# Hidden rows of three low-rank products kept in their PSUM banks

## The reference, cut to what matters

```python
def rwkv7_time_mix(h, ...):
    xx = token_shift(h) - h
    xr, xw, xk, xv, xa, xg = (h + xx * mu[j] for j in range(6))
    r = xr @ wr
    w_log = -jax.nn.softplus(-(w0 + jnp.tanh(xw @ w1) @ w2)) - 0.5
    k = xk @ wk
    v = xv @ wv
    a = jax.nn.sigmoid(a0 + (xa @ a1) @ a2)
    g = jax.nn.sigmoid(xg @ g1) @ g2
```

## Time and profile before

| what | value |
|---|---|
| time, median of 3 | 2699.92 us |
| lowest and highest | 2696.75 and 2700.97 us |
| the profiled execution | 2697.75 us |
| its span, first to last instruction | 2696.0 us |
| busy: PE, DVE, ACT, POOL | 2557.6, 1278.4, 740.1, 1479.3 us |
| mean granted clock of PE | 0.97 of full speed |

### The profile page before, as it was taken

One profiled execution on the slowest core, in us unless ns is written; L12 is line 12 of the kernel. 1 busy time (PEld: TensorE's weight loads), 2 busy tenths in 40 slices (PEclk: granted clock), 3 DMA queues, 4 the chain that ended last, 5 costly groups with the idle time before them and its releaser, 6 DMA issues. The chain is left out here.

```text
span 2696.0 us, 36707 instructions
## 1 busy us (share of the span) xinstructions
PE 2557.6 (95%) x15042; PEld 2039.6 (76%) x15042; DVE 1278.4 (47%) x1862; ACT 740.1 (27%) x1395; POOL 1479.3 (55%) x482
## 2 busy tenths in 40 slices
PE   5899988999999999999999998999799999999998
PEld 4677777788888796667888887777676568878787
DVE  7737336775662141453845526855075625131211
ACT  4643322231120212452311212322323423011210
POOL 3663632577777665205777772443373037754674
PEclk9999988999999999999999998999899999999999
DMA  6221424566562222103555522222253336222121
GB/s 268 98 82 53 128 78 169 237 236 230 222 230 96 87 101 78 54 1 136 219 203 219 211 100 99 90 106 94 94 187 111 125 148 237 105 77 71 70 97 75
DMA packets 89903, 358.80 MB, mean 133 GB/s; under 512 B 27288, under 2 KB 41112, under 8 KB 52384
## 3 DMA queue, kind: packets, MB, share of 16 engines
q1 hardware_dynamic: 64848, 227.12, 23.3%
q10 hardware_dynamic: 24912, 129.64, 12.8%
HBM read 317.66 MB, written 39.06 MB: 132 GB/s over the span
## 5 line engine op out<-in xcount | busy, mean ns | idle before, releaser
L499 POOL TENSOR_TENSOR whi<-wraw,con_sb 128x2048 fp32r<-128x2048 f32 x166 | 600.5, 3617 | 1002.8 <-PE ps L552 662.3
L501 POOL TENSOR_TENSOR wlo<-wraw,whi 128x2048 fp32r<-128x2048 f32 x166 | 782.6, 4715 | 13.0
L552 PE MATMUL ps<-hh,whi 128*128 128x512 f32 x952 | 372.9, 392 | 3.3 <-DVE hl L1930 3.3
L552 PE MATMUL ps<-hl,whi 128*128 128x512 f32 x952 | 371.5, 390 | 0.0
L552 PE MATMUL ps<-hh,wlo 128*128 128x512 f32 x952 | 371.4, 390 | 0.0
L552 PEld LDWEIGHTS ps<-hh,whi 128*128 128x128 f32 x952 | 179.4, 188 | 44.2 <-issue 3.7
L2155 DVE TENSOR_TENSOR midl<-rsq,midh 128x512 fp32r<-128x512 f32 x64 | 153.9, 2409 | 114.4 <-ACT midh L2112 114.4
L552 PEld LDWEIGHTS ps<-hh,wlo 128*128 128x128 f32 x952 | 179.4, 188 | 37.6
L552 PEld LDWEIGHTS ps<-hl,whi 128*128 128x128 f32 x952 | 179.5, 189 | 36.7
L552 PE MATMUL ps<-midh,whi 128*128 128x512 f32 x512 | 199.9, 391 | 0.0
L552 PE MATMUL ps<-midh,wlo 128*128 128x512 f32 x512 | 199.9, 390 | 0.0
(11 more groups left out here) (475 smaller groups left out, 4820.6 us busy)
## 6 DMA issues: line engine op xcount, KB each, us to landing
wraw<-wst SPq DMA_DIRECT2D x162, 1024.0 KB, 4.8
cond_w<-wcond ACTq DMA_DIRECT2D x68, 1024.0 KB, 4.8
first_w<-wcond SPq DMA_DIRECT2D x8, 1024.0 KB, 19.4
mod_w<-wcond SPq DMA_DIRECT2D x8, 1024.0 KB, 14.0
d_v<-ssb ACTq DMA_DIRECT2D x4, 1536.0 KB, 5.6
d_s<-ssb ACTq DMA_DIRECT2D x4, 1536.0 KB, 5.4
sld<-d_s SPq DMA_DIRECT2D x4, 1536.0 KB, 8.0
vld<-d_v SPq DMA_DIRECT2D x16, 384.0 KB, 3.9
```

The source lines that it names most:

```text
L499: pool.tensor_tensor(whi[:, s], wraw[:, f], C("zero").broadcast_to([P, BLK]), ALU.add).then_inc(sem("w_high"), 1)
L501: pool.tensor_tensor(wlo[:, s], wraw[:, f], whi[:, s].bitcast(F32), ALU.subtract).then_inc(w_split, 1)
L552: o = e.matmul(ps[:, b, :nt], w[:, k, mc], x[:, k0 + k, t0:t0 + nt], start=first and k == 0 and j == 0, stop=final and k == nk - 1 and j == 2)
```

## The change

The hidden rows no longer go to SBUF in full precision. ACT applies its function in place, from the bank to the same bank, then copies the bank's content rounded into `hidh` or `sgh`; DVE makes `hidl` or `sgl` from the bank and the high part. The bank is given back by DVE's subtraction (`hidden_low` raises `acc_free`), no longer by ACT's read. `hid` and `hidg` are gone, and with them ACT's two waits on `hid_ready`. PE, ahead of w2, waits for the banks of results 8 and 9 to be given back, which stands for both `hidl`.

```diff
-        hid, hidh, hidl = tiles("hid", 0, 1), tiles("hidh", 2, 1, F32R), tiles("hidl", 3, 1, F32R)
-        hidg, ksq = tiles("hidg", 0, 2), tiles("ksq", 0, 2)
+        hidh, hidl = tiles("hidh", 2, 1, F32R), tiles("hidl", 3, 1, F32R)
+        ksq = tiles("ksq", 0, 2)
...
                 full("g1", 1, 256, 5)
-                pe.wait_ge(*hid_ready.at(2))
+                for n in range(2):
+                    pe.wait_ge(*read_done(KT + n))
                 block_of(pe, firsts["w2"][1], 0, hidh, hidl, 1, BLK, mn=3)
...
-                def hidden_low(n, x, lo, hi):
+                def hidden_low(n, lo, hi, rows=slice(0, P)):
+                    b = (KT + n) % 3
                     dve.wait_ge(*hid_high.at(n + 1))
-                    dve.tensor_tensor(lo, x, hi.bitcast(F32), ALU.subtract).then_inc(*hid_ready.inc())
+                    dve.tensor_tensor(lo, ps[rows, b], hi.bitcast(F32), ALU.subtract).then_inc(acc_free[b], 1)
...
-                    hidden_low(n, hid[rr, 0], hidl[rr, 0], hidh[rr, 0])
+                    hidden_low(n, hidl[rr, 0], hidh[rr, 0], rr)
                 mixing_all(2, 1)
                 for n in range(2):
-                    hidden_low(2 + n, hidg[:, n], sgl[:, n], sgh[:, n])
+                    hidden_low(2 + n, sgl[:, n], sgh[:, n])
...
-                def hidden(x, func, hi, rows=slice(0, P)):
-                    read_out(x, func, rows=rows)
-                    act.wait_ge(*AC.last())
-                    act.activation(hi, x, ACT.Copy).then_inc(*hid_high.inc())
+                def hidden(func, hi, rows=slice(0, P)):
+                    b = bank()
+                    act.wait_ge(*AC.need(acc_ready))
+                    act.activation(ps[rows, b], ps[rows, b], func).then_inc(*hid_made.inc())
+                    act.wait_ge(*hid_made.at(hid_made.made))
+                    act.activation(hi, ps[rows, b], ACT.Copy).then_inc(*hid_high.inc())
+                    AC.up(acc_free[b])
...
                 hidden_half(1, ACT.Copy)
-                act.wait_ge(*hid_ready.at(2))
                 for n in range(2):
                     high(3)
-                    hidden(hidg[:, n], ACT.Sigmoid, sgh[:, n])
+                    hidden(ACT.Sigmoid, sgh[:, n])
                 high(2)
...
-                act.wait_ge(*hid_ready.at(4))
```

More of the change, by code:

```diff
@@ L846, in program @@
             mix_high, mix_ready = signal("mix_high"), signal("mix_ready")
-            hid_high, hid_ready = signal("hid_high"), signal("hid_ready")
+            hid_made, hid_high = signal("hid_made"), signal("hid_high")
             kk_squared, kk_summed = signal("kk_squared"), signal("kk_summed")
@@ L1075, in read_out @@
                     act.activation(dst, ps[rows, b], func, bias=bias).then_inc(*AC.up(acc_free[b]))
-                def hidden(x, func, hi, rows=slice(0, P)):
-                    read_out(x, func, rows=rows)
-                    act.wait_ge(*AC.last())
-                    act.activation(hi, x, ACT.Copy).then_inc(*hid_high.inc())
+                def hidden(func, hi, rows=slice(0, P)):
[5 more added lines that the diff above has]
+                    AC.up(acc_free[b])
                 def hidden_half(n, func):
                     rr = slice(64 * n, 64 * n + 64)
-                    hidden(hid[rr, 0], func, hidh[rr, 0], rr)
+                    hidden(func, hidh[rr, 0], rr)
                 def decays_of(g):
```

## The result

| | median | lowest to highest | runs |
|---|---|---|---|
| before | 2697.53 us | 2695.56 to 2700.97 | 12 |
| with the change | 2701.86 us | 2699.68 to 2709.0 | 12 |

The ratio is 1.0019 with a 95% interval of 1.0011 to 1.0027: 3 to 7 us slower, about 5. The ratio itself is just inside the 0.2% that the prediction called no change; its interval reaches beyond. The time lies in the predicted range (2696 to 2705.5), but the change was forecast at +0.6 us. So most of the difference, small as it is, has another cause than the sum named.

What follows compares the result with a forecast made beforehand. PE was taken as the bound, busy 2557.6 of 2696.0 us. A 4.38 us earlier gate read, against later bank return and half clock, summed to +0.6 us: 2698.4, or 2700.5 as a median; range 2696 to 2705.5.

Steps and rivals of the forecast that it cites:

- Parts 1 and 2: ACT's in-place functions and copies save 0; DVE's hidl from PSUM takes 0.68 us each, which alone gives PE nothing.
- Part 3: ACT, no longer waiting for hidl, reaches the gate's rows at 114.18 instead of 118.56 us: a gain of 4.38 us.
- Part 4: g1's banks return by DVE's subtraction behind j=2's eight tiles: 8.69 us from ACT's read to the first sgl.
- Part 5: PE's two idle pieces at w2 become one of 8.2 us, three half-clock matmuls follow; 0.55 us late at full clock.
- the upper bound: Half clock after PE resumes at w2 lasts 6.2 us, to 129.8 instead of 127.5: +1.8 us.
- Part 6: Everything behind w2 is carried along with PE's order; j=2's tiles finish at 123 instead of 127, wk gains nothing.
- Sum: All parts together over the whole kernel: +0.6 us, 2697.75 to 2698.4 for the profiled execution, 2700.5 for a median.
- The first: Rival: hidl from PSUM stays slow beside POOL, w2's third tile 5.5 us late; 2705 us, chance 0.10 including worse later clock.
- The second: Rival: PE's clock stays up or returns sooner around the w2 gap; -2 us, 2698, chance 0.06.
- The third: Rival: a PE wait behind 135.89 us, next near 186 and 196, gets shorter; 2694 us or less, chance 0.04.
- its last entry: Sign of a wrong prediction: w2's third tile starting more than 1.5 us after 123.81.

Runs made afterwards that it cites:

- e1: The changed kernel with DVE's first hidl moved up behind the fifth tile of j=5 instead of all eight; 2696.72 us, ratio 1.0000 to the kernel before.
- e3: The changed kernel with the rows of w1 and a1 read out to SBUF as before, only the gate's rows kept in their banks; 2701.54 us, ratio 1.0020.
- e6: e1 with the gate's two sgl subtractions moved up, behind the fourth and seventh tile of j=2; 2693.63 us, ratio 0.9985.
- e9: e7 with the gate's rows kept in their banks too and both sgl behind the fourth tile of j=2; 2689.47 us, ratio 0.9970.
- e8: The kernel before with only DVE's eight scans spread, one behind each tile of j=3; 2700.10 us, ratio 1.0007.
- e4: e1 with the gate's rows in SBUF, ACT's two gate reads back to back, five roundings of j=2 between its cum reads; 2698.86 us, ratio 1.0003.
- e7: e4 with DVE's eight scans put one behind each tile of j=3 instead of ahead of them; 2690.92 us, ratio 0.9972.

## Why the prediction was right or wrong, point by point

- *Parts 1 and 2* held. An in-place function took 0.57 to 0.58 us, the copy from PSUM 0.59 to 0.60. `hidl` took 0.67 and 0.70 us; in the changed kernel POOL was idle then, because of the very wait that was overlooked (it began its next block, which waits for g1's first matmul, at 108.57), but in e1 the second `hidl` took no longer beside POOL's work. The sentence in part 2 that this "by itself gives PE nothing" held as well.
- *The sentence from the Trainium skill* (VectorE: DVE Perf Modes, "The TRN2 errata") that a VectorE operation costs 62 cycles more from PSUM is not borne out: `sgl` from PSUM took 681 ns in the changed kernel, from SBUF 684.
- *Part 3* is the step that failed. ACT was free at 113.07 (113.0 said), but its read came at 119.49, not 114.18. The gain of 4.38 us rested on "the last matmul into g1's first bank starts at 113.76", taken over from the profile before, and this start depended on something that the change moves: g1 needs bank 2, given back before by ACT at 99.9 and now by the first `hidl` at 107.4. The prediction worked out who returns the banks that g1 fills and not who returns those that it needs. The diff's new line `then_inc(acc_free[b], 1)` applies to four results, 8 to 11; the prediction followed the last two to the tiles of w2 that take their banks, and did not follow result 8 to g1. That wait is worth 3.64 us and 1.45 us of half clock, 5.1 in all; e1 takes it out and the ratio goes from 1.0019 to 1.0000.
- *Part 4* held in its size: 8.62 us from ACT's read (119.49) to the first sgl (128.11), 8.69 said.
- *Part 5* held: one idle piece of 8.03 us (8.2 said), three matmuls at half clock in 1.45 us (128.84 to 130.29; 1.44 said). The clock came back later than at 127.5: in e1 the 6 us of the upper bound, +1.3 at wk instead of +0.55, still within the bounds (-2 to +1.8).
- *Part 6* held: everything behind is carried along, to within what the clock does. That the tiles of j=2 are finished early and wk gains nothing by it holds in e1 (their last low part starts at 122.42, and wk waits 0.30 us, for ACT's read of cum); in the changed kernel they are not early (127.50).
- *Sum.* +0.6 was said and about +5 measured (3 to 7); the missing term is the 5.1 of part 3. At wk, where it can be read without what the rest of the program adds, the changed kernel is 6.65 us late (142.54 against 135.89): 5.1 from g1, and most of the rest the 1.33 that e1 has too. It is luck that the forecast in us (2700.5) came as near as 1.4 to the measured median: the three first runs of before had a median 2.4 us above that of all twelve, and this hid more than half of what the sum had missed.
- *Rivals.* The first came out in price but not in mechanism: its condition, slow subtractions from PSUM, was not met, and e3 shows what slow subtractions do. The second did not occur: the clock was at 0.50 behind the gap. The third, a wait that gets shorter later, did not occur either; the waits near 186 and 196 changed by 0.2 us at most in the changed kernel.
- *Signs.* The prediction named "the sigmoid at 118" as a sign of the first rival. It came at 119.49, with `hidl` fast: the list of signs had no entry for a late g1. But its last entry fired: w2's third tile started 6.48 us after 123.81, and 1.5 was the limit. Wk's first matmul at 142.54 instead of 136.4 says the same.

That the order of DVE's list decides, and that keeping the rows in PSUM costs nothing that can be measured once the order is right, is shown by e6 and e9 against e1 and the change. What stays open is how much below 3 us the banks cost in e9, whether e8 is truly a little slower, and what sets the differences of up to 10 us behind 262 us between two executions of one kernel.

## What to carry to other kernels

When a change hands the return of a buffer from one engine to another, follow every use of that buffer in the ring, above all the one that takes it next, and not just the one whose wait the profile shows: a wait that is met for free in the trace of before has no row there. The position of the returning instruction in its engine's list counts for more than its duration: here 0.7 us of subtraction was cheap or cost 5 us with the same instructions. And where a step gets early, look at what it then runs beside: e4 lost its gain to eight scans, of which only the last had run beside POOL's next split until an earlier wk brought that split forward.

## What the runs showed of the hardware

- DVE instructions with two SBUF operands take longer beside POOL, and by amounts that vary: in the kernel before seven of the eight scans took 1.20 to 1.23 us each with POOL idle, and the last, beside POOL's split from 136.53 on, 4.56. All eight took 20.1 and 24.4 us in two executions of the same kernel e4, and 26.4 in e7. The subtraction for `hidl` took 1.76 and 5.00 us with both operands in SBUF, in the kernel before and again in e3; with one operand in PSUM it took 0.69 beside POOL in e1 (rows above). The Trainium skill, SBUF — State Buffer, "Who interferes with whom", says that a VectorE instruction with two SBUF inputs contends with a GpSimd instruction that reads SBUF, and that one with at most one, outside VectorE's two-port modes, doesn't contend; the traces agree (1.76 and 5.00 us against 0.69).
- The clock: behind 3.70 us of idleness it still stood at 1.00 in the profile before (119.20 to 120.50) and fell only in the next idle piece (0.50 from 121.0 to 123.8). In e8, behind 3.71 us of idleness at the same place, it was already at 0.50 (119.2 to 121.0), and ahead of g1 in the changed kernel it was down when PE went on after 3.64 us (0.56 on average from 107.6 to 110.9). So PE met either level behind idle pieces of the same length.
- A function in place, from a PSUM bank to the same bank, costs ACT the same as one to SBUF: 0.58 us (119.49 in the changed kernel) against 0.60 for the read of `hidg`.
